# Two passes instead of three for the weighted sums of the last attention branch, with a ScalarE and VectorE fold at the end

## The reference

```
def _banded_attention(q, k, v, window, sink=None):      # window 128, 16 query heads, 2 key/value heads of 64
    s = jnp.einsum('bnqkgd,bnjkd->bnkgqj', qb, kb) * (D ** -0.5)
    mask = ((diff >= 0) & (diff < window) & (key_pos[:, None, :] >= 0))[None, :, None, None]
    p = _masked_softmax(s, mask, sink_b)
    o = jnp.einsum('bnkgqj,bnjkd->bnqkgd', p.astype(vb.dtype), vb)
...
y_b = o_b.reshape(B, S, WIDTH_B) * jax.nn.silu(zb)
x = x + jnp.concatenate([y_a, y_b], axis=-1) @ w_out[l]
```

## Time and profile before

| what | value |
|---|---|
| median of 3 runs | 1964.39 us |
| profiled execution | 1965.28 us |
| its span, from the first to the last instruction | 1963.6 us |
| TensorE busy | 1874.1 us, 95% |
| weight loads busy (they overlap the matmuls) | 1540.5 us, 78% |
| VectorE busy | 1058.2 us, 54% |
| ScalarE busy | 675.5 us, 34% |
| mean granted TensorE clock | 0.984 of full speed |

### The profile page before, as it was taken

The page is one execution under the profiler, slowest core; times in us unless marked ns, Lnnn a source line. Parts: engine busy times, 40 slices in busy tenths (PEclk is TensorE's granted clock), DMA queues, the critical chain, the costliest instruction groups (busy, mean ns, idle before and its releaser), DMA issues.

```text
span 1963.6 us, 25766 instructions
## 1 busy us (share of the span) xinstructions
PE 1874.1 (95%) x9152; PEld 1540.5 (78%) x9152; DVE 1058.2 (54%) x1671; ACT 675.5 (34%) x1284; POOL 80.1 (4%) x75
## 2 busy tenths in 40 slices
PE   5999999999999899999969999999999999999994
PEld 3888888888888677678857887888888888887883
DVE  8633444443333767653358735665666666674334
ACT  5433333322222434332235224343433333352222
POOL 5000000000000000000024000000000000000002
PEclk9999999999999999999989999999999999999997
DMA  5322222222232322243223326211211222213332
GB/s 205 112 77 85 85 85 85 85 85 76 86 107 93 111 97 96 75 155 102 92 100 118 106 88 214 76 64 53 65 64 54 86 75 75 75 63 120 112 107 91
DMA packets 51774, 186.59 MB, mean 95 GB/s; under 512 B 6416, under 2 KB 6800, under 8 KB 50320
## 3 DMA queue, kind: packets, MB, share of 16 engines
q1 hardware_dynamic: 48528, 170.78, 26.2%
q0 software_dynamic: 3200, 15.21, 2.2%
HBM read 177.57 MB, written 8.39 MB: 95 GB/s over the span
## 4 chain that ended last, share of the span: by engine, by line
PE 87%; DVE 7%; ACT 2%; DVEq 1%; DMA 1%; issue 1%; ACTq 0%; SPq 0%
PE strip L397 23%; PE strip L399 23%; PE strip L398 23%; PE scores L397 3%; PE scores L399 2%; PE scores L398 2%; PE scores L446 2%; PE outputs L397 2%; PE outputs L399 2%; PE outputs L398 1%; DVE wl L1237 1%; DVE xl L1387 1%; DMA raw<-in_w 1%; PE odds L493 1%; PE scores L433 1%
## 5 line engine op out<-in xcount | busy, mean ns | idle before, releaser
L397 PE MATMUL strip<-xh,wh 128*128 128x512 f32 x2136 | 854.4, 400 | 44.6 <-DVE xl L1387 34.2
L399 PE MATMUL strip<-xh,wl 128*128 128x512 f32 x2136 | 835.5, 391 | 0.0
L398 PE MATMUL strip<-xl,wh 128*128 128x512 f32 x2136 | 835.2, 391 | 0.0
L397 PEld LDWEIGHTS strip<-xh,wh 128*128 128x128 f32 x2136 | 403.3, 189 | 137.0 <-DVE xl L1387 39.2
L399 PEld LDWEIGHTS strip<-xh,wl 128*128 128x128 f32 x2136 | 402.8, 189 | 86.0
L398 PEld LDWEIGHTS strip<-xl,wh 128*128 128x128 f32 x2136 | 403.5, 189 | 84.0 <-issue 4.1
L1237 DVE TENSOR_TENSOR wl<-raw,wh 128x1024 fp32r<-128x1024 f32 (+3 forms) x309 | 363.0, 1192 | 147.3 <-ACT wh L812 145.8
L812 ACT ACTIVATE wh<-raw 128x1024 fp32r<-128x1024 f32 (+3 forms) x309 | 308.4, 1022 | 76.2 <-PE strip L399 46.9
L834 ACT ACTIVATE prob<-scores,nms 128x128 f32<-128x128 f32 (+3 forms) x128 | 65.8, 526 | 160.5 <-DVE nms L1285 160.5
L1060 ACT ACTIVATE e_t<-o 128x512 f32 (+1 forms) x32 | 20.2, 632 | 240.1 <-DVE o L1641 120.3
L1283 DVE TENSOR_REDUCE nm<-scores 128x1 f32<-128x128 f32 (+3 forms) x128 | 58.8, 488 | 62.0 <-PE scores L433 58.5
(11 more groups left out here) (362 smaller groups left out, 1921.1 us busy)
## 6 DMA issues: line engine op xcount, KB each, us to landing
raw<-in_w SPq DMA_DIRECT2D x309, 512.0 KB, 3.3
xn<-o POOLq DMA_DIRECT2D x4, 1024.0 KB, 4.5
xr<-xn POOLq DMA_DIRECT2D x16, 256.0 KB, 3.0
out<-o SPq DMA_DIRECT2D x16, 256.0 KB, 2.3
o<-in_xt SPq DMA_DIRECT2D x3, 1024.0 KB, 11.9
xa<-in_xt POOLq DMA_DIRECT2D x3, 1024.0 KB, 8.3
o<-in_xt SPq DMA_DIRECT2D x2, 512.0 KB, 6.6
sel<-in_sel POOLq DMA_DIRECT2D x1, 1024.0 KB, 5.4
```

What stands on the lines that cost most here:

```text
L397: pe.matmul(out, ah, bh, start=first, stop=False, skip_group_check=shared)
L398: pe.matmul(out, ah, bl, start=False, stop=False, skip_group_check=shared)
L399: return pe.matmul(out, al, bh, start=False, stop=last, skip_group_check=shared)
```

## The change

Each value tile becomes one 128-column stationary `vst` that holds the hi values in columns 0 to 63 and the lo values in columns 64 to 127. Two matmuls, with `pth` and with `ptl`, replace the three. Head p now accumulates into the bank `po`, head p+8 into the bank `px` (named odds). In each bank partitions 0 to 63 hold the hi part and 64 to 127 the lo part of the sum, so the two halves have to be added: ScalarE copies `po[64:128]` to `halves[0:64]` and `px[0:64]` to `halves[64:128]`, VectorE adds `po[0:64]` and `px[64:128]` to them, and a third VectorE instruction multiplies by 0.5 and the gate. ScalarE waits for `pv_done` for this at the end of each pair; VectorE waits for the new semaphore `halved` instead of `pv_done`. The two memsets go, since every column of `vst` is written.

```diff
     kbb = pair("kbb", [P, S], offset=kv0)
-    vbz = (place("vbz_h", [P, 2, NQ, P], F32R, kv0 + 4096), place("vbz_l", [P, 2, NQ, P], F32R, kv0 + 8192))
+    vst = place("vst", [P, 2, NQ, P], F32R, kv0 + 4096)
+    halves = place("halves", [P, S], offset=kv0 + 8192)
...
                     cols = slice(BANDED * hh + WCOL[t], BANDED * hh + WCOL[t] + w)
-                    ins = three(pe, po[:, P * t:P * t + w], vbz[0][:, hh, t, :], vbz[1][:, hh, t, :],
-                                pth[:, cols], ptl[:, cols], hh == 0 and t == 0, hh == 1 and t == NQ - 1, True)
+                    out = (po, px)[hh][:, P * t:P * t + w]
+                    pe.matmul(out, vst[:, hh, t, :], pth[:, cols], start=t == 0, stop=False, skip_group_check=True)
+                    ins = pe.matmul(out, vst[:, hh, t, :], ptl[:, cols], start=False, stop=t == NQ - 1,
+                                    skip_group_check=True)
             ins.then_inc(pv_done, 1)
...
         pxv = px[:, :].rearrange("p (t d) -> p t d", t=NQ)
-        a.activation(vbz[0][:, 0, :, 0:64], pxv[:, :, 0:64], ACT.Copy)
-        a.activation(vbz[0][:, 1, :, 64:128], pxv[:, :, 64:128], ACT.Copy).then_inc(ev_act, 1)
+        a.activation(vst[:, 0, :, 0:64], pxv[:, :, 0:64], ACT.Copy)
+        a.activation(vst[:, 1, :, 0:64], pxv[:, :, 64:128], ACT.Copy).then_inc(ev_act, 1)
...
             if steps:
                 act_hi(a, u.on(5))
+            a.wait_ge(pv_done, 25 + p)
+            if not isinstance(p, int) or p > 0:
+                a.wait_ge(o_done, 24 + p)
+            a.activation(halves[0:64, :], po[64:128, :], ACT.Copy)
+            a.activation(halves[64:128, :], px[0:64, :], ACT.Copy).then_inc(halved, 1)
...
             if last:
-                v_.memset(vbz[0][:, :, :, :].bitcast(F32), 0.0)
-                v_.memset(vbz[1][:, :, :, :].bitcast(F32), 0.0)
                 take(v_, None, 1 - b, u(4), rb, yv[:, :])
...
-        v_.tensor_tensor(vbz[1][:, 0, :, 0:64], pxv[:, :, 0:64], vbz[0][:, 0, :, 0:64].bitcast(F32), ALU.subtract)
-        v_.tensor_tensor(vbz[1][:, 1, :, 64:128], pxv[:, :, 64:128], vbz[0][:, 1, :, 64:128].bitcast(F32),
+        v_.tensor_tensor(vst[:, 0, :, 64:128], pxv[:, :, 0:64], vst[:, 0, :, 0:64].bitcast(F32), ALU.subtract)
+        v_.tensor_tensor(vst[:, 1, :, 64:128], pxv[:, :, 64:128], vst[:, 1, :, 0:64].bitcast(F32),
                          ALU.subtract).then_inc(r_done, 1)
...
             if steps:
                 lo(v_, u.on(5))
-            head_out(v_, p + 24, o_at(p + 8), gate[:, :])
+            v_.wait_ge(halved, p + 1)
+            v_.tensor_tensor(halves[0:64, :], po[0:64, :], halves[0:64, :], ALU.add)
+            v_.tensor_tensor(halves[64:128, :], px[64:128, :], halves[64:128, :], ALU.add)
+            v_.drain()
+            v_.scalar_tensor_tensor(o_at(p + 8), halves[:, :], 0.5, gate[:, :], ALU.mult, ALU.mult).then_inc(o_done, 1)
```

More of the change, by code:

```diff
@@ L294, in _build @@
     scaled = sem("scaled")
+    halved = sem("halved")
     block = ctx.enter_context(nc.Block())
```

## The result

| | median | runs | profiled execution | its span | granted clock |
|---|---|---|---|---|---|
| before | 1964.51 us | 5, 1963.77 to 1966.28 | 1965.28 us | 1963.6 us | 0.984 |
| changed | 1973.01 us | 5, 1972.66 to 1974.69 | 1972.66 us | 1971.0 us | 0.982 |

The change makes the kernel slower: the ratio is 1.0043, with a 95% interval of 1.0029 to 1.0058. The prediction was 1973.4 us. Four more runs of the changed kernel, in a later group, gave 1975.9 us against 1964.7 for the kernel before beside them, 11.2 us more instead of 8.5; the experiments come back to this.

The account below looks back on a forecast made before the run. TensorE bounds the kernel; 10.6 us for pairs 1 to 6, 2.65 for pair 7, 2.65 for its end and 0.5 for clock, less 7.4 saved, give +9.0: 1974.3 profiled, 1973.4 median; 8-in-10 range 1969 to 1983.

Parts of the forecast that it names:

- Two passes save 0.92 a pair: Weighted sums on TensorE: two matmul passes instead of three save 0.46 us a head, 7.4 us over 8 pairs.
- The lateness D: VectorE's product and all behind it start later after the weighted sums, by 2.65 us, through ScalarE copies and VectorE additions.
- The hold rule: VectorE instruction starting in another group of 32 partitions waits for the one before; without it, additions 0.60 apart, not 0.70.
- estimate of 2.46 us: Two ScalarE copies and two VectorE operations in series by the skill's op costs; said to make the sum 1.5 us lower.
- about 3.1: Upper bound in us on VectorE's lateness behind the weighted sums, if copies and additions overlap nowhere.
- The room of 0.95 us: How late VectorE's last normalisation may get in a loop pair before TensorE waits at the transposes; none in pair 7.
- Pair 7: TensorE's wait for lo parts has no room, so it grows by 2.65 us, from 1.10 to 3.75.
- The end of pair 7: TensorE's wait for tile 15's lo part grows by 2.65 us, from 2.17 to 4.8.
- a clock that falls behind each new wait (1): Rival for TensorE's waits in six pairs: 10.2 us more, 1983.6, or 1978.5 for half the pairs; 22% in whole or part.
- Cheap operations on 64 partitions (2): Rival: 64-partition operations are cheaper, or copies and additions overlap, so D is 1.3 and the time 1962.6; 5%.
- Two passes that save little (3): Rival: stationary operand loads set the matmul distance on TensorE, so 3.8 us saved instead of 7.4, 1977.0; 7%.
- A D of 2.3 (4): Rival: the wait at a pair's end is partly hidden, or the copies start earlier; 1970.6 us; 13%.

Follow-up runs that it names:

- without the fold: Changed kernel without the ScalarE copies and VectorE additions, only the bank of head p multiplied by the gate; 1958.9 us, ratio 0.9967 to the kernel before.

## Why the prediction was right

The mechanism is as it was said: less work on TensorE, a longer chain on VectorE, waits at the places named. That the median came within 0.4 us is partly luck. The sum said 9.0 us, and the profiled executions are 7.4 apart, because one term was 1.6 us too large and others were off by less. The changed kernel's profiled execution was then the fastest of its five runs, 0.35 below the median, where the forecast had put it 0.9 above, as before; that made 8.5. Its own steps, one by one:

- Two passes save 0.92 a pair: 0.93 measured from pair 0 to pair 1, where nothing else differs, and 7.32 in all without the fold. The memsets cost nothing to lose: the branch began 0.35 us earlier, less than the runs differ there by.
- The lateness D was put at 2.65 and is 2.76. ScalarE started 0.12 behind the sums, not 0.15. Its two copies don't overlap: 0.61 from start to start, not 0.48. The row that I took the overlap from has copies of 256 elements to the same partitions, these have 512 and go to different ones. The length isn't it: before, two `pth` copies to the same partitions, of 512 elements (0.593) and 384 (0.495), took 0.96 together, so they overlapped too. That the start partition makes the difference fits, but no run tests it. The additions stand 0.70 apart as foreseen, the product follows after 0.17.
- The hold rule that I had weighed for the additions ("VectorE: DVE Perf Modes", "Two Vector instructions with no wait between them", of the Trainium skill): the distance of 0.70 between them agrees with it, against 0.60 or 0.61 between the product and the next lo part.
- Two figures of the prediction's working don't hold. It set the estimate of 2.46 us for the four operations in series against D = 2.65 and made the sum 1.5 us lower by it. Its own four terms (0.48, 0.59, 0.70, 0.69) are 2.46 as well; the rest of D is the 0.03 between the engines and the 0.16 of the register. So that estimate gives the same sum. And the bound "about 3.1" adds up to 2.96, or 2.99 with the 0.03. Neither is in the forecast.
- The room of 0.95 us held: 2.76 - 0.95 is 1.81, TensorE's idle rows say 1.65, since a matmul of 512 columns is shown as 0.39 long where the next starts after 0.23: its shown end lies 0.16 behind that. With the restart each of the six pairs lost 0.97 + 0.93 = 1.90; I had 1.76, 0.8 us less in all.
- Pair 7: its wait grew from 1.10 to 3.85, by 2.75 (2.65 was said). The clock fell to 0.56 behind it and cost nothing in the end: the wait of 1.12 us further on took the loss up and is gone. I had put 0.5 us for it.
- The end of pair 7: the wait grew by 2.70, but the program from there is only 1.04 longer. This was the term that was furthest off. I had written the clock there as neither gain nor loss; before, eight matmuls ran at the lower level behind the second wait, at full cost; in the changed profile the matmuls at the lower level came ahead of that wait, which hid them, and the eight ran at 1.00. That is 1.7 us to the good. It is not dependable. In the second profile of the changed kernel the matmuls at the lower level stood on both sides of the wait, as the next two rows show, and from the end of the sums to the end of the program it took 3.2 us more than before:

```profile
1788.40:1791.90 3.50, 2.92 (x6) 1.82 (x6) 3.34 (x4) 1.11 (x2) 0.00 (x0) 0.50 0.65 217
1792.00:1795.50 3.50, 3.50 (x8) 2.81 (x9) 2.00 (x3) 1.89 (x3) 1.07 (x2) 0.50 0.83 279
```

- Together: -7.4 + 11.4 + 2.75 + 1.04 - 0.35 = 7.4 us between the profiled executions; the sum said 9.0, the medians differ by 8.5.

Of the rivals, a clock that falls behind each new wait (1) didn't show: 1.00 in all stretches with a wait of 1.65. Cheap operations on 64 partitions (2) fell with the rows of 0.60 and 0.68. Two passes that save little (3) fell with the kernel without the fold, 7.32 us less. A D of 2.3 (4) fell with the 2.76. But for the third, the rows that show the forecast's terms are the rows in which these would have been seen.

## What to carry to other kernels

An instruction that is taken off the busiest engine and paid for on idle ones is only free if the payment doesn't stand ahead of something that the busiest engine will wait for: ask for its place in the queue and the room of the chain behind it, not for the idle share. Here the same instructions cost 1.9 us in each of six pairs ahead of the row maxima, and nothing in the loop behind them. Measure the room by making the chain longer in steps, on the old kernel, before the change is written.

## What the runs showed of the hardware

- Operations on 64 partitions took as long as on 128: 0.60 us for a ScalarE copy of 512 elements out of PSUM, 0.68 for a VectorE addition.
- Two ScalarE copies to different start partitions stood 0.61 us apart, the length of one; two to the same partitions had overlapped by 0.11 (256 elements each) and 0.13 (512 and 384). What makes the difference was not tested.
- Single waits of 1.65 us, 29.6 us apart, left TensorE's clock at 1.00; waits of 3.85 and 4.87 were followed by 0.50 to 0.56. Two waits of about 2 us, 3.6 us apart, were followed by 0.51 in one kernel (2.17 and 1.94) and by 1.00 in another (2.17 and 1.97).
- How long the lower level lasts behind the same wait of about 3.8 us differed: 7, 9 and 14 matmuls, counting those partly at the lower level, in four profiles (14 in two of them). The time of one kernel differs from run to run too: the last branch began between 1545.8 and 1551.9 us in thirteen profiles of eleven kernels though the work ahead of it is the same but for two memsets, and one kernel's runs (the product made twice) gave 1966.2 to 1974.1. A difference of 2 or 3 us between kernels has to be looked for in the trace, in the stretch that was changed.
